# Units on both sides of every norm in halves of the tokens, low parts of the weights in place, three units resident

## The chip, the cores and the metric

The kernel runs on one core of a Trainium2 chip. The metric is the device time of one execution in microseconds (us). Five engines work side by side, each through its own list of instructions in order: TensorE (PE; its weight loads are shown apart as PEld), VectorE (DVE), ScalarE (ACT), GpSimd (POOL), and SyncE (SP), which here only starts DMAs.

## The reference

The input is one sequence of 512 tokens of width 1024. Three layers follow each other: layer a (forgetting attention, then a convolutional FFN), layer b (differential attention, then a convolutional FFN) and layer c (a gated mix of grouped attention and a state-space branch, then a gated FFN). Cut to the parts around the norms:

```
x = layer_norm(1.414 * x + attention_a(x));  x = layer_norm(1.414 * x + ffn(x))     # norms a0, f0
x = layer_norm(1.414 * x + attention_b(x));  x = layer_norm(1.414 * x + ffn(x))     # norms a1, f1
h = rms_norm(x) @ w_in_2                                                            # norm c0
x = x + rms_norm(mixed @ w_out)                                                     # norm m
h2 = rms_norm(x) @ w_gate_up;  x = x + rms_norm((silu(gate) * up) @ w_down)         # norms p and f
```

A layer norm subtracts the mean of a token over its 1024 values, divides by the root of the variance plus 1e-5, and applies a gain and an offset. An rms norm divides by the root of the mean square plus 1e-6 and applies a gain. There are eight norms, at six places: f1 is followed at once by c0, and m at once by p. The inputs and the result are float32.

## The kernel before

**Layout and precision.** An activation lies in SBUF as eight blocks of 128 features by 512 tokens. Each is split into a high part in a short float format (`XH`) and the rest (`XL`). A weight is split likewise: `RAW` is what the DMA brings, ACT rounds it to `HI` (L1530), and DVE or POOL subtracts to get `LO` (the helper at L1899 on DVE, at L2382 on POOL). A product is three matmuls: HI with XH, HI with XL, LO with XH. One such matmul has 128x128 stationary values and 512 moving columns, or 256 where the unit is of kind `mt` (tokens stationary, weights moving).

**Units.** All the weights are cut into units of up to 8 blocks of 128 rows by 256 columns (1 MB), taken in one fixed order (`unit_sequence`). Two units are resident: `RAW`, `HI` and `LO` have two buffers each (`i % 2`). SP loads unit i once HI and LO of unit i-2 are made (`load_raw`, L1195). While PE multiplies with unit i-1, unit i is split in up to four parts (`split_steps`, `part_step`); its first HI waits until PE is done with unit i-2.

**Order.** `agenda()` writes one list of steps. Each engine walks through it and picks out its own instructions, so this list is the order on every engine. `tick` counts matmul steps; it lets `chore()` advance background generators by one `yield`, and lets the attention run beside the units.

**Around a norm before.** The last units before a norm produce eight blocks `YH`, one after the other (`residual`, or the copy `cye`). After each, `accumulate` squares it on ACT (L1548) and adds the squares, and where there is a mean also the block, on POOL (L2402, L2404). When all are done, `statistics` sums over the features on PE: a matmul of a 128x128 piece with a single column, four token groups for each buffer (`stat0`); then small operations on DVE and ACT (`stat1`, `stat2`, L1937 to L1945, L1557 or L1560); then matmuls that spread the mean and the reciprocal over all partitions (`stat1`, `stat3`). Then for each block of 512 tokens: DVE subtracts and multiplies (L1953, L1956; for an rms norm one operation), ACT applies gain and offset (L1566) and rounds to `XH` (L1570), POOL makes `XL` (L2382). The first unit after the norm waits for XL block by block. At c0 and p a second norm of this kind comes before it. The last norm f ends with `fin`: DVE multiplies (L1970), DVE or POOL adds (L1978, L2504), SP stores.

In the trace all matmuls of the helper have line L1239, and the tiles tell them apart: `PS<-XH,HI` and the like are unit matmuls, `PS<-NEGC,FP` is the one that clears the bank of the sums and is the first of `stat0`, `PS<-FP,A_a` and `PS<-FP,SQ_a` are the sums, `PS<-FP,TN` the spreading. In the suffixes a stands for a0 and a1, f for f0 and f1, m, p and c for the norms of those names. A matmul of plain float32 values has two records.

```
def statistics(n, mean):
    at_bank(put("stat0", n, mean), 6)
    if mean:
        at_bank(put("stat1", n), 5)
    put("stat2", n, mean)
    put("stat3", n, mean)
def layer_norm(n, final=None):
    statistics(n, True)
    for j in range(8):
        s = put("ln", n, j)
```

## Time and profile before

| | us |
|---|---|
| median of 3 runs (lowest, highest) | 2441.58 (2437.21, 2452.46) |
| the profiled execution, whole | 2443.44 |
| its span, first to last instruction | 2441.6 |
| PE busy | 2254.6 (92%) |
| DVE busy | 1096.0 (45%) |
| ACT busy | 1001.4 (41%) |
| POOL busy | 974.8 (40%) |
| DMA queue q1 | 181.27 MB, 21.5% of 16 engines |

The profile is of one execution. Busy time is the union of an engine's instructions. A matmul's duration in it is longer than the distance to the next, because matmuls overlap; the rate of PE is read from start to start.

### The profile page before, as it was taken

What the parts mean: (1) busy time and instruction counts of PE and PEld (TensorE: products, weight loads), DVE (VectorE), ACT (ScalarE), POOL (GpSimd) and SP (SyncE); (2) the same over time, 40 slices, a digit from 0 to 9 for tenths busy, and PEclk for the clock granted to TensorE, in tenths of its full rate; (3) what the DMA queues carried; (4) which work ended last, traced back from release to release, by engine and by line L of the source; (5) the groups of instructions that cost most, each with busy time, mean ns of one, the idle gap of its engine ahead of it and who ended that gap; (6) DMA issues with size and microseconds to landing.
All of it is one profiled execution on the core that took longest, in us unless ns stands there. A gap on an engine that the chain in (4) does not pass through costs nothing.

```text
span 2441.6 us, 28073 instructions
## 1 busy us (share of the span) xinstructions
PE 2254.6 (92%) x10880; PEld 1841.6 (75%) x10880; DVE 1096.0 (45%) x1774; ACT 1001.4 (41%) x2015; POOL 974.8 (40%) x760
## 2 busy tenths in 40 slices
PE   7999999999979887999999789996899997999997
PEld 6778778888867776788888666664687885888886
DVE  3545555553345764555443333546545234232222
ACT  5665454443254553444442244443344234232222
POOL 3554644333455641644334351103423345232232
PEclk9999999999989998999999887997999997999998
DMA  4111222222212220222322111110012221222221
GB/s 152 51 65 58 70 87 91 100 101 95 97 61 75 77 83 18 70 101 90 104 97 95 59 46 35 35 35 18 18 44 95 86 104 52 104 87 104 97 95 50
DMA packets 29844, 183.07 MB, mean 75 GB/s; under 512 B 3984, under 2 KB 4112, under 8 KB 11920
## 3 DMA queue, kind: packets, MB, share of 16 engines
q1 hardware_dynamic: 29712, 181.27, 21.5%
q8 instruction: 87, 1.43, 0.2%
q14 instruction: 45, 0.37, 0.0%
HBM read 174.97 MB, written 2.10 MB: 73 GB/s over the span
## 4 chain that ended last, share of the span: by engine, by line
PE 84%; DVE 5%; ACT 4%; POOL 4%; issue 2%; DMA 1%; SPq 0%; POOLq 0%; ACTq 0%; DVEq 0%
PE PS L1239 82%; PE PS L1332 1%; POOL LO L2382 1%; POOL XL L2382 1%; PE PS L1442 1%; DVE bQS L1899 1%; DVE cCVT L2266 0%; DVE aQS L1899 0%; DMA RAW<-wall 0%; POOL A_p L2402 0%; POOL bROT L2430 0%; ACT bP L1739 0%; POOL A_c L2402 0%; PE PS L1380 0%; POOL bTQ L2435 0%
## 5 line engine op out<-in xcount | busy, mean ns | idle before, releaser
L2382 POOL TENSOR_TENSOR LO<-RAW,HI 128x512 fp32r<-128x512 f32 (+1 forms) x382 | 542.3, 1436 | 686.9 <-ACT HI L1530 686.9
L1239 PE MATMUL PS<-XH,HI 128*128 128x512 f32 (+1 forms) x1584 | 645.1, 407 | 40.7 <-POOL XL L2382 20.5
L1239 PE MATMUL PS<-XH,LO 128*128 128x512 f32 (+1 forms) x1584 | 628.1, 397 | 0.0
L1239 PE MATMUL PS<-XL,HI 128*128 128x512 f32 (+1 forms) x1584 | 628.1, 397 | 0.0
L1899 DVE TENSOR_TENSOR LO<-RAW,HI 128x512 fp32r<-128x512 f32 (+3 forms) x286 | 313.5, 1102 | 290.9 <-ACT HI L1530 290.7
L1530 ACT ACTIVATE HI<-RAW 128x512 fp32r<-128x512 f32 (+3 forms) x668 | 365.1, 608 | 170.6 <-PE PS L1239 167.2
L1239 PEld LDWEIGHTS PS<-XH,HI 128*128 128x128 f32 (+1 forms) x1584 | 303.7, 192 | 132.5 <-issue 57.3
L1239 PEld LDWEIGHTS PS<-XH,LO 128*128 128x128 f32 (+1 forms) x1584 | 302.9, 191 | 66.6 <-issue 1.1
L1239 PEld LDWEIGHTS PS<-XL,HI 128*128 128x128 f32 (+1 forms) x1584 | 304.2, 192 | 58.4 <-issue 1.0
L1239 PE MATMUL PS<-HH,HI 128*128 128x512 f32 x528 | 205.4, 389 | 0.0
L1239 PE MATMUL PS<-HL,HI 128*128 128x512 f32 x528 | 205.4, 389 | 0.0
L1239 PE MATMUL PS<-HH,LO 128*128 128x512 f32 x528 | 205.4, 389 | 0.0
L2418 POOL TENSOR_TENSOR UT<-UT 128x512 f32<-128x512 f32 x44 | 56.4, 1282 | 204.8 <-ACT UT L1591 204.8
L1239 PE MATMUL PS<-HI,XH 128*128 128x256 f32 (+1 forms) x416 | 125.7, 302 | 11.3 <-DVE aVL L1899 2.8
L1589 ACT ACTIVATE UT<-PS,SM 128x512 f32<-128x512 f32 x88 | 67.7, 772 | 131.4 <-PE PS L1239 131.4
L1239 PE MATMUL PS<-HI,XL 128*128 128x256 f32 (+1 forms) x416 | 119.4, 287 | 0.0
L1239 PE MATMUL PS<-LO,XH 128*128 128x256 f32 (+1 forms) x416 | 119.4, 287 | 0.0
L1239 PEld LDWEIGHTS PS<-HH,HI 128*128 128x128 f32 x528 | 99.1, 188 | 20.7
L1239 PEld LDWEIGHTS PS<-HH,LO 128*128 128x128 f32 x528 | 99.1, 188 | 20.6
L1239 PEld LDWEIGHTS PS<-HL,HI 128*128 128x128 f32 x528 | 99.1, 188 | 20.4
L1987 DVE SCALAR_TENSOR_TENSOR UT<-PS,SM,UT 128x511 f32<-128x511 f32 x88 | 65.4, 743 | 91.8 <-ACT UT L1589 91.8
L2424 POOL TENSOR_SCALAR aP<-aP,aRC 128x128 f32<-128x128 f32 (+1 forms) x64 | 69.3, 1084 | 92.0 <-DVE aRC L2068 91.8
(380 smaller groups left out, 3352.3 us busy)
## 6 DMA issues: line engine op xcount, KB each, us to landing
RAW<-wall SPq DMA_DIRECT2D x138, 1024.0 KB, 4.8
RAW<-wall SPq DMA_DIRECT2D x24, 896.0 KB, 4.4
bROT<-bTQ SPq DMA_DIRECT2D x64, 64.0 KB, 2.0
RAW<-wall SPq DMA_DIRECT2D x5, 512.0 KB, 3.2
XF<-xT SPq DMA_DIRECT2D x4, 512.0 KB, 6.0
outT<-XR SPq DMA_DIRECT2D x8, 256.0 KB, 2.0
FP<-cfp SPq DMA_DIRECT2D x1, 1024.0 KB, 6.8
MKF<-cmask SPq DMA_DIRECT2D x1, 704.0 KB, 11.4
```

The source lines that it names most:

```text
L1239: return e.matmul(out, a, b, start=start, stop=stop)
L1332: m = e.transpose(PS[bank][:, 128 * kb:128 * kb + 128], aP[:, 512 * (n % 4) + 128 * kb:512 * (n % 4) + 128 * kb + 128], IDN)
L1442: m = e.transpose(PS[bank][:, 128 * kb:128 * kb + 128], p[:, 128 * kb:128 * kb + 128], IDN)
L1530: act(HI[i % 2][:, c], RAW[i % 2][:, c], ACT.Copy).then_inc(SEM["hi"], 1)
L1589: act(x, PS[ag.tiles[t].bank][:, :], ACT.Identity, bias=col(f"cb{lay}", f), scale=col(f"cw{lay}2", f)).then_inc(SEM["ui"], 1)
L1899: return e.tensor_tensor(out, x, h.bitcast(F32), ALU.subtract)
L1987: e.scalar_tensor_tensor(out=x[:, 1:512], in0=ps[:, 0:511], scalar=col(f"cw{lay}1", f), in1=x[:, 1:512], op0=ALU.mult, op1=ALU.add).then_i ...
L2382: return e.tensor_tensor(out, x, h.bitcast(F32), ALU.subtract)
L2418: e.tensor_tensor(g, g, v, ALU.mult).then_inc(SEM["um"], 1)
L2424: e.tensor_scalar(p, p, aRC[:, n:n + 1], None, ALU.mult).then_inc(SEM["dg"], 1)
```

## The change

**Three units resident.** `LO` gets the addresses of `RAW`: the subtraction writes over its own input. The 48 KB hold three units then. SP loads unit i when PE is done with unit i-3, and the first HI of unit i waits for the same.

**Halves before a norm** (`ending`). The last units are multiplied for tokens 0 to 255 first, all of them, and then for tokens 256 to 511. At a0, a1 and m these are the last three units of four; at f0, f1 and f the last group of three long units (22 blocks of rows). A matmul has 256 moving columns there; both 128-column halves of a unit share one PSUM bank. In the long group the bank is cleared first by a matmul of float32 zeros with 512 columns (one for each half).

**Halves after a norm** (`beginning`). The first units take tokens 0 to 255 of all, then 256 to 511: two units in layers a and b (for b `bqk` 0 and `bv` 0, whose banks are now 2 and 3 in place of 0 and 1), three at c0 (`ck`, `cq` 0, `cq` 1) and three at p.

**The norm in between** (`chain`, `two_norms`) is a background generator, one for each half of the tokens, advanced by `chore()` as the units go on. `st0` sums over the features: POOL's running sums (`acc`) cover only the blocks before the halved units, and the halved blocks are summed by PE itself, each piece of 128x128 by a single-column matmul, for the squares and, where there is a mean, for the values. `stq` does so in c0 and p, for all eight blocks. `stb` spreads. Then pairs of blocks by 256 tokens are normalised (`lnp`, `lnr`, `rmp`, `n1`, `fin`), as many elements in an instruction as before.

`LATE` and `STATS` are the numbers of chore turns between the end of a half and its sums, and between the sums and the spreading. `HOLD` delays the splitting of the next unit. `XR` is moved to another address.

```diff
+HOLD = 16
+LATE = 4
+STATS = 4
...
+    def ending(n, groups, src, banks, evict, chain):
...
+        for f in range(2):
+            for (p, keys), bank in zip(groups, banks[f]):
...
+                    for k, q in rows:
+                        step_of("mh", t, kk + k, q)
+                        tick(0.5)
...
+                freed[bank] = evict(p, t, f)
+                put("acch", n, p, f)
+                at_slot(steps[-1], "P", p - 1, ("ssum", ("st0", n, f)))
+            together_chores.append(chain(f))
...
+    def beginning(units, last=False):
...
+        def known(kk, f):
+            while x_step[kk][f] is None:
+                assert chores or together_chores
+                chore()
...
+    def chain(n, f, mean, each, begun=False):
+
+        if not begun:
+            for _ in range(LATE):
+                yield
+            while bank_of_norm(n, f) in norm_at:
+                yield
+            norm_at.add(bank_of_norm(n, f))
+            s = put("st0", n, f)
+            at_bank(s, bank_of_norm(n, f))
+        put("st1", n, f)
+        for _ in range(STATS):
+            yield
+        s = put("stb", n, f)
+        b = bank_of_norm(n, f)
+        freed[b] = ("spr", s)
+        for p in range(4):
+            freed[b] = yield from each(f, p)
+        norm_at.discard(b)
...
+            s2 = put("sqp", n2, f, p)
+            at_slot(s2, "S", None, ("ssum", ("stq", n2, f, p)))
+            yield
+            yield
+            s2 = put("stq", n2, f, p)
...
+        ending(n, [(i, [(name, i)]) for i in (1, 2, 3)], src, [[2, 3, 4], [7, 0, 1]], residual_half(n), layer_norm(n))
...
+        ending(n, [(3, [("dn" + lay, 3, p) for p in range(3)])], "H" + lay, [[4], [7]], evict, chain)
...
+        beginning([("mm", ("bqk", 0), (128, 128), [0, 1], qk_evac(0)), ("mt", ("bv", 0), None, [2, 3], v_evac(0))])
...
+        beginning([("mm", ("ck", 0), (128,), [0], qk_evac(4)), ("mm", ("cq", 0), (128, 128), [1, 2], qk_evac(0)),
+                   ("mm", ("cq", 1), (128, 128), [3, 4], qk_evac(2))], last=True)
...
-    HI = [sb(f"HI{i}", 2048, F32R, base + 16 * K + 8 * K * i) for i in range(2)]
-    LO = [sb(f"LO{i}", 2048, F32R, base + 32 * K + 8 * K * i) for i in range(2)]
+
+    RAW = [sb(f"RAW{i}", 2048, F32, base + 8 * K * i) for i in range(3)]
+    LO = [sb(f"LO{i}", 2048, F32R, base + 8 * K * i) for i in range(3)]
+    HI = [sb(f"HI{i}", 2048, F32R, base + 24 * K + 8 * K * i) for i in range(3)]
...
+            if i >= 3:
+                e.wait_ge(*when_(ag.unit_end[i - 3]))
...
+                        if q == 0:
+                            mm(PS[T.bank][:, :], IDN, NEGC[:, 8:9].to_broadcast([128, 512]), True, False)
...
+            elif kind == "st0":
+                n, f = a
+                nb, mean = NORM[n], n in MEANED
+                e.wait_ge(*when("cd", "cst"))
+                mm(PS[bank][:, 0:4], IDN, NEGC[:, 8:12], True, False)
...
+                for c in range(2):
+                    t = slice(256 * f + 128 * c, 256 * f + 128 * c + 128)
+                    mm(PS[bank][:, c:c + 1], nb["A2"][:, t], MEAN[:, 0:1], False, False)
+                    if mean:
+                        mm(PS[bank][:, 2 + c:3 + c], nb["A1"][:, t], MEAN[:, 0:1], False, False)
+                for p in pairs_of[n]:
+                    if mean:
+                        e.wait_ge(*y_half(n, p, f))
+                        for q in range(2):
+                            for c in range(2):
+                                y = blk(YH, 2 * p + q)[:, 256 * f + 128 * c:256 * f + 128 * c + 128]
+                                mm(PS[bank][:, 2 + c:3 + c], y, MEAN[:, 0:1], False, False)
+                    e.wait_ge(*when("sq", "acch", n, p, f))
+                    for q in range(2):
+                        for c in range(2):
+                            y = nb[f"P{p - 1}"][:, 256 * q + 128 * c:256 * q + 128 * c + 128]
+                            done = mm(PS[bank][:, c:c + 1], y, MEAN[:, 0:1], False, p == pairs_of[n][-1] and q == 1 and c == 1)
...
+            elif kind == "stb":
...
+                if n in MEANED:
+                    for c in range(2):
+                        mm(ps[:, 128 * c:128 * c + 128], SUMS[f][:, 2 + c:3 + c].to_broadcast([128, 128]), IDN)
+                for c in range(2):
+                    done = mm(ps[:, 256 + 128 * c:384 + 128 * c], RSD[f][:, c:c + 1].to_broadcast([128, 128]), IDN)
```

## Rows read from the trace of the kernel before

**Rows 1.** The page: busy time by engine; PE's clock in 40 slices.
```profile
PE 2254.6 (92%) x10880; PEld 1841.6 (75%) x10880; DVE 1096.0 (45%) x1774; ACT 1001.4 (41%) x2015; POOL 974.8 (40%) x760
...
PEclk9999999999989998999999887997999997999998
```

**Rows 2.** Timeline around norm f0: start us, length us, engine, line, tiles, [idle <-releaser].
```profile
672.01 0.39 PE L1239 MATMUL PS<-HH,HI 128*128 128x512 f32 x1
...
676.09 0.39 PE L1239 MATMUL PS<-HH,HI 128*128 128x512 f32 x1
...
676.77 0.28 PE L1239 MATMUL PS<-NEGC,FP 128*128 128x8 f32 x2
...
692.55 0.69 DVE L1953 TENSOR_TENSOR T_f<-PS,YH 128x512 f32<-128x512 f32 x1 [3.00 <-PE PS L1239]
...
695.55 2.65 POOL L2382 TENSOR_TENSOR XL<-T_f,XH 128x512 fp32r<-128x512 f32 x2 [14.18 <-ACT XH L1570]
...
696.97 0.77 PE L1239 MATMUL PS<-XH,HI 128*128 128x512 f32 x1 [4.45 <-POOL XL L2382]
...
701.37 0.44 PE L1239 MATMUL PS<-XL,HI 128*128 128x512 f32 x1
```

**Rows 3.** Timeline of PE around norms f1 with c0, and m with p.
```profile
1379.38 0.28 PE L1239 MATMUL PS<-NEGC,FP 128*128 128x8 f32 x2
...
1416.76 0.77 PE L1239 MATMUL PS<-XH,HI 128*128 128x512 f32 x1 [2.95 <-POOL XL L2382]
```
```profile
2029.53 0.28 PE L1239 MATMUL PS<-NEGC,FP 128*128 128x8 f32 x2
...
2058.00 0.77 PE L1239 MATMUL PS<-XH,HI 128*128 128x512 f32 x1 [2.95 <-POOL XL L2382]
```

**Rows 4.** Timeline of PE around norms a0 and a1.
```profile
302.56 0.28 PE L1239 MATMUL PS<-NEGC,FP 128*128 128x8 f32 x2
302.97 1.95 PE L1239 MATMUL PS<-FP,A_a 128*128 128x1 f32 x16
304.77 1.18 PE L1239 MATMUL PS<-FP,YH 128*128 128x1 f32 x8
...
316.22 0.76 PE L1239 MATMUL PS<-XH,HI 128*128 128x512 f32 x1 [4.46 <-POOL XL L2382]
```
```profile
1006.57 0.28 PE L1239 MATMUL PS<-NEGC,FP 128*128 128x8 f32 x2
...
1018.35 0.76 PE L1239 MATMUL PS<-XH,HI 128*128 128x512 f32 x1 [4.46 <-POOL XL L2382]
```

**Rows 5.** Timeline at the end, behind the last unit matmul; the last addition.
```profile
2419.65 0.28 PE L1239 MATMUL PS<-NEGC,FP 128*128 128x8 f32 x2
...
2428.08 0.75 DVE L1970 SCALAR_TENSOR_TENSOR YH<-YH,SM,PS 128x512 f32<-128x512 f32 x1 [2.17 <-PE PS L1239]
...
2437.95 1.26 POOL L2504 TENSOR_TENSOR XR<-XR,YH 128x512 f32<-128x512 f32 x1 [1.29 <-DVE YH L1970]
```

**Rows 6.** Windows: stretch, us, busy by engine, PEclk, DMA share, GB/s.
```profile
304.00:305.00 1.00, 1.00 (x12) 1.00 (x11) 0.17 (x1) 0.78 (x2) 0.00 (x0) 1.00 0.59 246
...
306.00:307.00 1.00, 1.00 (x6) 1.00 (x6) 0.00 (x0) 0.33 (x2) 0.00 (x0) 0.50 0.00 0
```

**Rows 7.** Timeline of PE: matmuls of 256 columns (unit bv), and of float32.
```profile
918.98 0.28 PE L1239 MATMUL PS<-LO,XH 128*128 128x256 f32 x1
...
920.05 0.28 PE L1239 MATMUL PS<-LO,XH 128*128 128x256 f32 x1
```
```profile
1699.14 1.95 PE L1239 MATMUL PS<-FP,cBC 128*128 128x512 f32 x4 [0.88 <-DVE FP L2329]
```

**Rows 8.** Waits of PE from 705 to 735, behind norm f0: sum, times, longest.
```profile
PE PS L1239 <- DVE bVL L1899: 5.4, 1, 5.4
PE PS L1239 <- ACT bTQ L1707: 2.0, 1, 2.0
```

**Rows 9.** Waits of ACT over the whole span: sum, times, longest.
```profile
ACT HI L1530 <- PE PS L1239: 167.2, 26, 7.6
```

More of the change, by code:

```diff
@@ L163 @@
     "res": (("res", 1),),
[L164 to L170 removed]
+    "resh": (("res", 1),),
+    "acch": (("sq", 1),),
+    "sqp": (("sq", 1),),
+    "stq": (("ssum", 1),),
+    "st0": (("ssum", 1),),
+    "stb": (("spr", 1),),
+    "lnp": (("lt", 1), ("la", 1), ("xh", 1), ("xl", 1)),
+    "lnr": (("lt", 1), ("la", 1)),
+    "rmp": (("lt", 1), ("xh", 1), ("xl", 1)),
     "ue": (("ui", 2), ("ud", 2), ("us", 1), ("um", 1), ("hh", 1), ("hl", 1)),
@@ new lines, in beginning @@
+    def beginning(units, last=False):
+        ts = []
+        def known(kk, f):
+            while x_step[kk][f] is None:
+                assert chores or together_chores
+                chore()
+        held = None
+        for f in range(2):
+            for q, (kind, key, widths, banks, evac) in enumerate(units):
+                if not f:
+                    i = take(key)
+                    if last and q == len(units) - 1:
+                        held, due[0] = due[0], None
+                    rows = [(i, k) for k in range(places[key][1])]
+                    ts.append((len(tiles), rows))
+                    if kind == "mm":
+                        for j, w in enumerate(widths):
+                            tiles.append(Tile(rows, sum(widths[:j]), w, banks[j], "X"))
+                    else:
+                        for c in range(4):
+                            tiles.append(Tile(rows, 0, places[key][2], banks[c % len(banks)], "X", c))
+                            tiles[-1].half = c // 2
+                t0, rows = ts[q]
+                if kind == "mm":
+                    for kk in range(len(rows)):
+                        known(kk, f)
+                        for j in range(len(widths)):
+                            step_of("mm", t0 + j, kk, f)
+                            tick(0.5)
+                    if f:
+                        for j in range(len(widths)):
+                            evac(j, t0 + j)
+                else:
+                    for c in (2 * f, 2 * f + 1):
+                        for kk in range(len(rows)):
+                            known(kk, f)
+                            step_of("mt", t0 + c, kk)
+                            tick(0.5)
+                        freed[tiles[t0 + c].bank] = evac(c, t0 + c)
+                if held is not None and f and q == len(units) - 2:
+                    due[0], due[1], held = held, 0.0, None
@@ L512, in rms_apply @@
-    def rms_apply(n):
-        statistics(n, False)
-        for j in range(8):
-            x_step[j] = put("rms", n, j)
-            freed[6] = ("lt", x_step[j])
+        s = put("acc", n, j, mean)
+        if j:
+            at_slot(s, "S", None, ("ac", s))
+    def chain(n, f, mean, each, begun=False):
[16 more added lines that the diff above has]
+        norm_at.discard(b)
@@ new lines, in bank_of_norm, with normed, each, layer_norm @@
+    def bank_of_norm(n, f):
+        return 6 - (f if n not in ("c0", "p") else 1 - f)
+    def normed(n, kind):
+        def each(f, p):
+            s = put(kind, n, f, p)
+            at_slot(s, "T", None, ("xl", s))
+            x_step[2 * p][f] = x_step[2 * p + 1][f] = ("xl", s)
+            yield
+            yield
+            return ("lt", s)
+        return each
+    def layer_norm(n):
+        return lambda f: chain(n, f, True, normed(n, "lnp"))
+    def two_norms(n, n2):
+        def each(f, p):
+            if n == "f1":
+                s = put("lnr", n, f, p)
+                at_slot(s, "T", None, ("la", s))
+            else:
+                s = put("n1", n, f, p)
+            s2 = put("sqp", n2, f, p)
+            at_slot(s2, "S", None, ("ssum", ("stq", n2, f, p)))
+            yield
+            yield
+            s2 = put("stq", n2, f, p)
+            if p == 0:
+                norm_at.add(bank_of_norm(n2, f))
+                at_bank(s2, bank_of_norm(n2, f))
+            return ("lt", s)
+        def both(f):
+            yield from chain(n, f, n == "f1", each)
+            yield from chain(n2, f, False, normed(n2, "rmp"), True)
+        return both
@@ new lines, in scalar @@
+                dst = buf(n, "S", step) if j else NORM[n]["A2"]
+                act(dst[:, :], blk(YH, j), ACT.Square).then_inc(SEM["sq"], 1)
+            elif kind == "acch":
+                n, p, f = a
+                e.wait_ge(*y_half(n, p, f))
+                if ag.slot_free[step] is not None:
+                    e.wait_ge(*when_(ag.slot_free[step]))
+                act(by2(buf(n, "P", step)[:, :]), pair(YH, p, f), ACT.Square).then_inc(SEM["sq"], 1)
+            elif kind == "sqp":
+                n, f, p = a
+                e.wait_ge(*(when("la", "lnr", "f1", f, p) if n == "c0" else when("n1", "n1", "m", f, p)))
+                if ag.slot_free[step] is not None:
+                    e.wait_ge(*when_(ag.slot_free[step]))
+                act(by2(buf(n, "S", step)[:, :]), pair(XR, p, f), ACT.Square).then_inc(SEM["sq"], 1)
+            elif kind == "st0":
@@ L1578, in scalar @@
                 act(blk(YH, j), PS[ag.tiles[t].bank][:, :], ACT.Copy).then_inc(SEM["cye"], 1)
+            elif kind == "cyeh":
+                n, p, t, f = a
+                e.wait_ge(*when_(ag.tiles[t].full))
+                act(pair(YH, p, f), by2(PS[ag.tiles[t].bank][:, :]), ACT.Copy).then_inc(SEM["cye"], 1)
             elif kind == "ue":
```

549 lines of the change are left out of this document (303 added, 246 removed).

## The prediction

> **What bounds the kernel now.** I read the page first. PE is busy 92% of the span and the other engines 40 to 45% [rows 1]; the clock line shows nines but for a few slices, so PE runs near its full clock of 2.4 GHz and nothing else is close to being the bound. So time can come only from PE: its holes, its slow stretches, and the work given to it. The rate of that work is read in the timeline from start to start: six times three matmuls of 512 columns start between 672.01 and 676.09, which is 0.227 us each [rows 2]. PE is dense like this over all the FFN parts.
>
> Next, the timeline of PE at each norm. From the row that clears the bank of the sums to the first `PS<-XH,HI` there pass 13.7 us at a0 and 11.8 at a1 [rows 4], 20.2 at f0 [rows 2], 37.4 at f1 with c0 and 28.5 at m with p [rows 3]: 111.6 us. Behind it the clock is low for a while: at f0 ten matmuls take 4.40 us (696.97 to 701.37) and not 2.27, so 2.1 us are lost [rows 2]; at five places 10.6. At the end 22.0 us lie between the last unit matmul and the end of the span, 2441.6 - 2419.65 [rows 5]. Sum of what the norms cost: **144.2 us**. One more hole hangs on the place behind f0: PE waits 2.0 us for a bank that holds `bqk` 0 and 5.4 us for one that holds `bv` 0 [rows 8].
>
> **The change, part by part.**
>
> *Removed.* If everything were covered, the 122.2 us at five places go, and the end is worked out below. The two waits behind f0, 7.4 us, should go: `bv` gets banks 2 and 3, and `bqk` 1 then takes banks that were emptied a whole half unit earlier. Bounds 0 (DVE is late for another bank) and 10 (the slow clock behind the wait goes too). I take 7.4.
>
> *Narrower matmuls.* Nine matmuls of 256 columns start between 918.98 and 920.05, in 1.07 us: 0.119 each [rows 7]. Two of them against one of 0.227 cost 0.011 more. Halved are, before norms, 3 units x 48 matmuls at a0, a1 and m (432) and 22 blocks x 2 x 3 = 132 at f0, f1 and f (396); behind norms 96 at each of a0 and a1, 48 for `bqk` 0, 120 at c0, 144 at p (504). `bv` has 256 columns already. 1332 x 0.011 = **14.7 us**. Bounds: 0, and 1332 x 0.025 = 33 if short accumulations run worse than `bv`.
>
> *Sums on PE.* This is the part that costs. A single-column matmul of float32 takes (304.77 - 302.97) / 8 = 0.225 us [rows 4], as long as a whole unit matmul of 512 columns, since its price is the weight load. Before, POOL added seven of eight squares and PE needed 16 sums and a clearing matmul for a layer norm, 9 for an rms norm. Those are inside the holes counted above. Now `st0` needs, for each half at a0 and a1, 1 + 4 + 3 x 8 = 29; at f0 and f1 1 + 4 + 8 = 13; at m 1 + 2 + 3 x 4 = 15; `stq` at c0 and p 1 + 4 x 4 = 17; f 7. `stb` adds 4 for a layer norm and 2 for an rms norm; I price these as the others (a bound above is 0.35). For both halves: a0 and a1 66 each, f0 and f1 34 each, c0 and p 38 each, m 34, and f's first half 9. 319 x 0.225 = **71.8 us**, on PE's path because the lists run in order. The clearing with 512 float32 columns: two matmuls are the four records of 1.95 us [rows 7], some 0.95 each after the overlap; two at f0, f1 and f each, 6 x 0.95 = **5.7 us**.
>
> *The end.* From the first multiplication of `fin` at 2428.08 to the last addition's end at 2439.2 pass 11.1 us for eight blocks [rows 5]. The second half is four pairs, the same work by halves: 5.6 saved. Sums and spreading halve too, about 2.9 less. 22.0 - 8.5 = **13.5 us** remain. Bounds 11 and 17.
>
> *Waits that stay.* One turn of `chore` is two steps, six matmuls of 256 columns: 0.71 us. From the spreading to the first XL the old chain needs 692.55 to 696.97, 4.4 us [rows 2], and POOL makes an XL in 1.33 (2.65 for two), DVE needs two operations of 0.69 for a pair, ACT about as much. So pairs come every 1.5 to 1.7 us. Behind a0: five turns 3.6, sums 6.5, four turns 2.9, spreading 0.9, 4.4: 18.3 us, against a first half of two units of 11.4 plus the 7.4 that PE itself spends on sums and spreading. It fits; a pair is used up in 1.4 us, so 2 us at a0 and a1 each and 1 at f0. At c0 it does not fit. `stq` of a pair stands only two turns (1.4 us) behind the pair's `lnr`, yet DVE, ACT and the square need 3.2: 1.8 us of standing in each half, with the unit matmuls queued behind it on PE. Then `ck` is narrow, a pair feeds 0.7 us of work while pairs come every 1.5, and the spreading comes right ahead of the units: some 4.6 us in each half. Together 12.8. At m with p the halves are longer; 4.4. Sum **22 us**, bounds 8 and 45: DVE, ACT and POOL also split the next units meanwhile, and each waits in order.
>
> *The clock.* In the trace PE goes down to 1.2 GHz with no hole ahead: between 302.97 and 308 it does single-column matmuls one after the other and is busy throughout, and the granted clock is 1.00 in 304 to 305 and 0.50 in 306 to 307 [rows 4, 6]. So it falls about 3 us into such a run. `st0` at a0 and a1 is a run of 29 x 0.225 = 6.5 us in each half. Its rest of 3 us would take twice as long, and a little is lost behind it: 3.6 us, four times, 14.4. At f0, f1 and m the runs are 2.9 to 3.4 us, and it will fall in some of six: 4. Behind the standing at c0 and p, 5.6. Sum **24 us**, bounds 0 and 40. The Trainium skill, "TensorE: Matmul & The Clock Gate", section "Why this matters for your kernels", asks only that there be no idle gaps between bursts of matmuls. By that rule dense sums would keep the clock, and the change would remove what lowered it; this trace does not agree at a0, where PE was not idle.
>
> *Three units resident.* ACT waits 167.2 us for PE in front of HI [rows 9], but all 26 waits are of up to 7.6 us beside dense matmuls, and PE waited for no LO worth naming. Loads of 1 MB have a whole unit's time as before. Subtracting in place is as much work. Nothing: bounds -5 and +5.
>
> *Sum.* Removed 122.2 + 22.0 + 7.4 = 151.6. Added 14.7 + 71.8 + 5.7 + 13.5 + 22 + 24 = 151.7. Net 0.1 on the profiled execution's 2443.4; that stands 1.9 above the median of 2441.6, so the forecast is **2442 us**.
>
> **The rivals.**
>
> *A. Dense sums keep the clock* (also the skill's rule above). For it: at f0 the slow matmuls stand right behind holes [rows 2], which the change fills, and the units are dense on both sides of each sum; against it the rows at a0 [rows 4, 6]. Then 24 us fewer: 2418, and with waits at their lower bound 2404.
>
> *B. PE stands at the sums in every half: slower.* The mechanism is the order of the list: a sum or a spreading put at a fixed number of turns stands ahead of the unit matmuls on PE, and DVE, ACT and POOL come to it late because the splitting of units, now at twice the rate (5.7 us a unit and not 10.9), is queued ahead of it. It decides once squares come over 3.6 us behind the end of a half. There are 14 half chains ahead of f; at 2.3 us each, standing and clock, 32 more: 2474. For it: a unit's split is four subtractions as wide as the one that takes POOL 1.33 us [rows 2], two of them or more on POOL, so POOL alone spends 2.7 of those 5.7 us, beside the XL. Against: they are 40 to 45% busy on the whole [rows 1].
>
> *C. The halves do not overlap with the chain.* The beginning of a unit pumps `chore` until its block is known, and this empties the turns without any matmul between. It can only bite at c0 and p, since elsewhere the turns suffice. Price 10 more at each: 2462.
>
> **Chances.** Forecast 0.48, A 0.24, B 0.16, C 0.12. The likeliest gives 2442. Its own range is 2425 to 2460 (the bounds of the waits and the clock half used). The range for 8 in 10 reaches to both sides: **2406 to 2472**. A measurement of this kernel can tell about 1% from no change. Faster by over 1% (under 2417): half of A, a lower tail of the forecast and of an end that shrinks more, 0.29. Slower by over 1% (over 2466): B mostly, part of C and of the forecast's upper tail, 0.23. Within 1%: 0.48.
>
> **What would show it.** In the changed profile: PE's busy share rises to some 96% with the span unchanged. Single-column matmuls number over twice as many, at 0.225 us where the clock is full. At a0 and a1 the windows show a clock of 0.50 inside or just behind `st0`, with PE busy. The time from the last full-width matmul of `ao` 0 to the first of `up` 2, less its unit matmuls at 0.119, is above the 15 us that norm a0 cost before: the layer norms behind attention lose some 10 us each, f0 wins about 17, m with p a few, and the end 6 to 8. PE waits for POOL XL only at `ck`. The forecast is wrong if the clock stays at 1.00 through `st0`, if the waits of PE in the transitions sum to over 45 us, or if the matmuls of 256 columns start more than 0.125 us apart.

## The result, and the profile after

The change makes the kernel slower: 2489.03 us against 2444.22 for the kernel before in the same session (medians of four runs each; 2478.86 to 2489.78 and 2437.21 to 2452.46). The ratio is 1.017, with a 95% interval of 1.013 to 1.0215. On a second chip it was 2487.46 against 2436.59, ratio 1.0207 (1.0178 to 1.0236). The forecast was 2442 in a range up to 2472; the loss is 46 us of span in the profiled executions (2487.8 against 2441.6). One of the nine executions of a later run, `h1_both`, took 2627.63 us at a granted clock of 0.82 and is left out of that run's numbers.

The page of the kernel after: busy time by engine, PE's clock, the chain of waits by engine.

```profile
span 2487.8 us, 31338 instructions
PE 2332.1 (94%) x12565; PEld 1972.8 (79%) x12576; DVE 1101.3 (44%) x1826; ACT 1014.5 (41%) x2061; POOL 917.1 (37%) x718
...
PEclk9999999999999898899999886996899999999999
...
PE 84%; DVE 5%; ACT 4%; POOL 3%; issue 2%; DMA 0%; another core or an unknown queue 0%; SPq 0%; POOLq 0%; ACTq 0%; DVEq 0%
```

Against [rows 1], PE is busy 77.5 us more and the span is 46 longer, so about 31 us of holes went. They were filled with work, and with slow work. The time that PE is busy at half clock grew from 185.7 to 222.2 us, which costs half of the difference, 18; so 59 of the 77.5 us are work at full clock, and 59 + 18 - 31 is the 46. The table says where: I compared the starts of the same marks in both traces (first `PS<-aOH,HI`, first `PS<-HH,HI` of each FFN, called `HH` 0 to 2, first and last `bQS`, first `cMXH`, the end). The third column is the prediction's own working, its terms sorted by place.

| stretch | after minus before, us | by the prediction's terms |
|---|---|---|
| norm a0 | +14.5 | +10.9 |
| norm f0, to the first `bQS` | -9.6 | -15.8 |
| attention b, first to last `bQS` | +5.9 | 0 |
| norm a1 | +14.5 | +12.8 |
| f1, c0 and part c up to `cMXH` | +22.7 | -1.7 |
| m and p | +1.4 | -2.7 |
| f and the end | -3.1 | -3.1 |

They sum to 46.3 (the kernel after is 0.2 ahead at the first mark) and 0.4. Half of the miss is one row, f1 with c0 and part c.

**Norm a0.** The timeline of PE in the kernel after, then windows of the same stretch (stretch, us, busy by engine, PEclk, DMA share, GB/s).

```profile
292.18 0.28 PE L1441 MATMUL PS<-NEGC,FP 128*128 128x4 f32 x2
292.31 1.03 PE L1441 MATMUL PS<-FP,A_a 128*128 128x1 f32 x8
...
295.00 1.55 PE L1441 MATMUL PS<-FP,YH 128*128 128x1 f32 x8
296.41 1.84 PE L1441 MATMUL PS<-FP,P_a 128*128 128x1 f32 x8
...
299.82 1.84 PE L1441 MATMUL PS<-FP,P_a 128*128 128x1 f32 x8
```
```profile
290.00:295.00 5.00, 5.00 (x47) 5.00 (x45) 0.20 (x1) 2.12 (x3) 0.00 (x0) 1.00 0.01 3
295.00:300.00 5.00, 5.00 (x27) 5.00 (x27) 0.00 (x0) 0.00 (x0) 0.00 (x0) 0.53 0.00 0
300.00:303.00 3.00, 3.00 (x15) 3.00 (x16) 0.65 (x4) 0.30 (x1) 0.00 (x0) 0.50 0.00 0
303.00:306.00 3.00, 3.00 (x17) 3.00 (x17) 0.26 (x1) 0.00 (x0) 0.00 (x0) 0.57 0.01 3
```

Two records are one sum. Four sums take 0.90 us from 292.31 and 1.70 from 296.41. PE has no hole in this stretch, it is busy 16 of 16 us, and the granted clock goes from 1.00 to 0.50 some 3 us into the run of 29 sums, as it did behind [rows 4]; it stays there for 10.2 us, beyond the end of the sums (in the second half for 6.8). This is what the prediction priced at 3.6 us in each half.

**Norm c0.** The same two views of the kernel after.

```profile
1407.15 0.28 PE L1441 MATMUL PS<-NEGC,FP 128*128 128x4 f32 x2
1409.18 1.05 PE L1441 MATMUL PS<-FP,S_f 128*128 128x1 f32 x8 [1.74 <-ACT S_f L1795]
...
1411.69 1.70 PE L1441 MATMUL PS<-FP,S_f 128*128 128x1 f32 x8
...
1415.96 1.70 PE L1441 MATMUL PS<-FP,S_f 128*128 128x1 f32 x8
...
1430.32 0.35 PE L1441 MATMUL PS<-XH,HI 128*128 128x256 f32 x1 [2.80 <-POOL XL L2646]
...
1434.59 0.55 PE L1441 MATMUL PS<-XH,HI 128*128 128x256 f32 x1 [3.32 <-POOL XL L2646]
```
```profile
1405.00:1410.00 5.00, 3.26 (x30) 3.17 (x29) 3.97 (x7) 2.60 (x5) 0.00 (x0) 1.00 0.28 98
1410.00:1415.00 5.00, 5.00 (x31) 5.00 (x31) 1.27 (x2) 4.27 (x9) 0.00 (x0) 0.65 0.00 0
1415.00:1420.00 5.00, 5.00 (x25) 5.00 (x25) 0.00 (x0) 0.00 (x0) 0.00 (x0) 0.50 0.55 187
1420.00:1425.00 5.00, 5.00 (x25) 5.00 (x25) 0.49 (x2) 0.57 (x2) 0.00 (x0) 0.50 0.06 23
```

The waits are where the prediction put them: PE stands 1.74 us for the square of the first pair (the prediction said 1.8), and for POOL's XL behind the spreading. From 1395 to 1474 they sum to 12.9 us (9.4 for XL, 3.5 for squares), against 12.8 predicted. The clock is what differs. Behind the stand of 1.74 us it falls, and then PE does 13.7 us of dense work of layer 1 at half speed, unit matmuls with three groups of sums between them, with no hole in it (x25 records in 5 us; 47 in the window at full speed above).

**Behind f0.** PE in attention b, then ACT at the same time, in the kernel after.

```profile
761.76 0.23 PE L1441 MATMUL PS<-MK 128*128 128x128 bf16 x1
768.52 1.01 PE L1441 MATMUL PS<-bQS 128*128 128x384 f32 x2 [6.53 <-ACT bP L1993]
```
```profile
741.53 0.63 ACT L1766 ACTIVATE HI<-RAW 128x512 fp32r<-128x512 f32 x1 [4.42 <-DMA RAW<-wall]
...
765.08 1.27 ACT L1979 ACTIVATE bQS<-bTQ 64x512 fp32r<-64x512 f32 x2 [4.55 <-POOL bTQ L2695]
766.36 1.28 ACT L1993 ACT_TABLE_LOAD   x1
767.66 0.37 ACT L1993 ACTIVATE bP<-PS,bST 128x128 f32<-128x128 f32 x1
```

The two waits of [rows 8] are gone, and a new one of 6.53 us stands 35 us later, for the first exponential. Two things ahead of it on ACT could be the cause: the stand of 4.42 us for a load, and the one of 4.55 us for POOL in the conversion of the rope. Run `h3_load_first` moves the first.

**The end.** Last sums and last addition of the kernel after, the partner of [rows 5].

```profile
2474.80 0.28 PE L1441 MATMUL PS<-NEGC,FP 128*128 128x4 f32 x2
...
2483.80 1.26 POOL L2764 TENSOR_TENSOR XR<-XR,YH 128x512 f32<-128x512 f32 x1 [1.41 <-DVE YH L2237]
```

From the last unit matmul to the end of the span pass 13.1 us (2487.8 - 2474.7), where 13.5 were predicted.

### The profile page after: what moved, and what is told of

Its sections match the earlier page's. It is cut to its first block, busy times and chain, and to the rows that moved or that the text cites. A ratio compares the mean times of both kernels' runs of the same rounds, so it can differ in the third digit from the quotient of the medians.

```text
span 2487.8 us, 31338 instructions
## 1 busy us (share of the span) xinstructions
PE 2332.1 (94%) x12565; PEld 1972.8 (79%) x12576; DVE 1101.3 (44%) x1826; ACT 1014.5 (41%) x2061; POOL 917.1 (37%) x718
## 4 chain that ended last, share of the span: by engine, by line
PE 84%; DVE 5%; ACT 4%; POOL 3%; issue 2%; DMA 0%; another core or an unknown queue 0%; SPq 0%; POOLq 0%; ACTq 0%; DVEq 0%
PE PS L1441 82%; POOL LO L2646 1%; PE PS L1568 1%; PE PS L1678 1%; POOL XL L2646 1%; DVE aQS L2153 0%; ACT bP L1993 0%; DVE LO L2153 0%; ACT HI L1766 0%; DVE bQS L2153 0%; PE PS L1616 0%; POOL A_f L2666 0%; ACT bQS L1979 0%; ACT T_a L1815 0%
## 5 line engine op out<-in xcount | busy, mean ns | idle before, releaser
L1441 PE MATMUL PS<-XH,HI 128*128 128x512 f32 (+2 forms) x1752 | 675.2, 385 | 40.1 <-POOL XL L2646 20.1
L1441 PE MATMUL PS<-XL,HI 128*128 128x512 f32 (+2 forms) x1752 | 657.0, 375 | 0.0
L1441 PE MATMUL PS<-XH,LO 128*128 128x512 f32 (+2 forms) x1752 | 656.7, 375 | 0.0
L1441 PEld LDWEIGHTS PS<-XH,HI 128*128 128x128 f32 (+1 forms) x1752 | 337.7, 193 | 117.4 <-issue 39.4
L1766 ACT ACTIVATE HI<-RAW 128x512 fp32r<-128x512 f32 (+3 forms) x668 | 365.9, 607 | 97.4 <-DMA RAW<-wall 96.9
L1441 PEld LDWEIGHTS PS<-XH,LO 128*128 128x128 f32 (+1 forms) x1752 | 337.6, 193 | 58.5 <-issue 1.1
L1441 PEld LDWEIGHTS PS<-XL,HI 128*128 128x128 f32 (+1 forms) x1752 | 338.3, 193 | 51.8 <-issue 1.0
L1441 PE MATMUL PS<-HH,HI 128*128 128x512 f32 (+1 forms) x660 | 235.7, 357 | 3.3 <-POOL LO L2646 3.2
L1441 PE MATMUL PS<-HL,HI 128*128 128x512 f32 (+1 forms) x660 | 231.9, 351 | 0.0
L1441 PE MATMUL PS<-HH,LO 128*128 128x512 f32 (+1 forms) x660 | 231.8, 351 | 0.0
L1441 PEld LDWEIGHTS PS<-HH,HI 128*128 128x128 f32 x660 | 128.2, 194 | 21.0 <-POOL LO L2646 3.6
L1441 PEld LDWEIGHTS PS<-HL,HI 128*128 128x128 f32 x660 | 128.2, 194 | 16.9 <-issue 1.4
L1441 PEld LDWEIGHTS PS<-HH,LO 128*128 128x128 f32 x660 | 128.2, 194 | 15.4
L1842 ACT ACTIVATE UT<-PS,SM 128x512 f32<-128x512 f32 x88 | 67.5, 771 | 126.4 <-PE PS L1441 126.4
```

What stands on the lines that cost most here:

```text
L1441: return e.matmul(out, a, b, start=start, stop=stop)
L1766: act(HI[i % 3][:, c], RAW[i % 3][:, c], ACT.Copy).then_inc(SEM["hi"], 1)
L1842: act(x, PS[ag.tiles[t].bank][:, :], ACT.Identity, bias=col(f"cb{lay}", f), scale=col(f"cw{lay}2", f)).then_inc(SEM["ui"], 1)
```

## The experiments

Every ratio is to the kernel before, run on the same chip in the same session. "The marks" are those of the table above.

**e1_resident: three units resident, alone.** In the kernel before, three buffers each of RAW and HI, LO in RAW's place, and the waits that go with them:

```
-                    e.wait_ge(s_raw[i % 2], 16 * (i // 2 + 1))
-                    if i >= 2:
-                        e.wait_ge(*when_(ag.unit_end[i - 2]))
+                    e.wait_ge(s_raw[i % 3], 16 * (i // 3 + 1))
+                    if i >= 3:
+                        e.wait_ge(*when_(ag.unit_end[i - 3]))
```

> The kernel before with the three resident units alone: LO written over RAW, loads and the first HI of unit i waiting for PE's end of unit i-3; no halves. Theory (residency is free): within 5 us of before, 2439 to 2449. Rival (ACT now stands at HI for the load, in front of its other work, and this is what the attention parts of the changed kernel lost): 8 to 15 us slower, with ACT's waits for the DMA of RAW near 97 us as in the changed kernel.

Measured: 2444.08 us, ratio 1.0026 (1.0002 to 1.005), span 2442.3 against 2441.6. All the marks lie within 3 us of those before. By the profiles this part costs 0.6 us, by the ratio 6 (0.5 to 12), by the medians 10 (2434.2 before in that session). The rival's sign is there: ACT waits 108.9 us for the loads of `RAW` (96.9 in the kernel after). Its 8 to 15 us are neither shown nor excluded. It is not what made most of the 46.

**e2_narrow: only narrower matmuls.** In the kernel before, all 66 `up` units as matmuls of 256 columns, 3168 becoming 6336 (`three` is the kernel's three matmuls on a range of columns):

```
+                    if ag.order[i][0] in ("up0", "up1", "up2"):
+                        m = three(kk, w, slice(0, 256), start, stop)
+                        if stop:
+                            for q in range(8):
+                                m = three(q, slice(q * n + T.c, q * n + T.c + T.w), slice(256, 512), q == 0, q == 7)
```

> The kernel before with all 66 `up` units in matmuls of 256 columns, tokens 0 to 255 of a tile first and then the rest: 3168 matmuls become 6336, nothing else is changed. My prediction's term (0.011 us for each halved matmul): 35 us more, 2479. Rival (the matmuls in the halves cost 0.1235 us, 0.020 each): 63 us more, 2507. If width cost nothing: 2444.

Measured: ratio 1.0231 (1.0186 to 1.0275), 56 us, close to the rival's 63 and not to 35. Over 3168 that is 0.018 us for each halved matmul; by the marks the three layers cost 17.4, 19.3 and 15.6 us over 1056 each, 0.015 to 0.018. The prediction took 0.011 from nine starts in a row of `bv`. Within a row it was nearly right: in `up0` of e2 twenty starts from 400.06 take 2.40 us, 0.120 each, so a halved matmul costs 0.013. The rest comes between the rows (layer 0 has 2.1 us more holes). In the kernel after, the unit matmuls of 256 columns stand 0.123 us apart on average (clock and holes taken out). So the term of 14.7 us is 17 by the rows and **24** by e2's ratio.

**e3_fewer_sums: fewer sums at a0 and a1.** In the kernel after; the sums of the first two halved pairs of a0 and a1 are left out of the statistics, 13 in place of 29 in each half:

```
                 for p in pairs_of[n]:
+                    if n in ("a0", "a1") and p != pairs_of[n][-1]:
+                        continue
```

> The changed kernel, leaving out of the sums of norms a0 and a1 the halved blocks of units 1 and 2 (16 of 29 single-column matmuls in each half; the values of these norms are then those of fewer blocks). Theory (each sum costs 0.225 us of PE, and a run of 29 also brings the clock down over dense work): 64 x 0.225 = 14.4 us for the sums and some 10 for the clock, 24 less than the changed kernel, 2465. Rival (the clock falls for another reason, the sums alone count): 14 less, 2475. Rival (sums hide under other waits): under 6 less.

Measured: 2469.25 us, ratio 1.0134 (1.0108 to 1.016), between my theory's 2465 and the rival's 2475. Over the kernel before of its own session it is 35 us, where the kernel after is 45 and 51 (`e0_after_again`): 10 to 16 us less. The sums themselves are 64 x 0.225 = 14.4, so the times alone don't show that the clock counts. The trace does: half clock over matmuls is 3.4 us at each of a0 and a1, where the kernel after has 17.1 and 13.7, worth 12. By the marks of this execution, which was 8 us faster than the run's median, a0 costs 1.0 us over the kernel before and not 14.5, a1 2.7 and not 14.5: 25.3 us less. Windows of e3, for comparison with those of a0 above:

```profile
295.00:300.00 5.00, 5.00 (x37) 5.00 (x37) 0.65 (x4) 0.30 (x1) 0.00 (x0) 0.79 0.00 2
300.00:303.00 3.00, 3.00 (x22) 3.00 (x22) 1.38 (x2) 0.03 (x1) 0.00 (x0) 0.77 0.17 22
303.00:306.00 3.00, 3.00 (x27) 3.00 (x27) 2.81 (x5) 2.00 (x4) 0.00 (x0) 1.00 0.81 328
```

The clock still falls, for 3.4 us and not 10.2.

**e4_probe: the same sums in dense work.** In the kernel before, single-column matmuls put between the unit matmuls of `up`: four runs of 29 in layer 0, four of 13 in layer 1, sixteen of 4 in layer 2 (they add work and take none away):

```
+    if name in plan and j in plan[name][1] and T.c == 0 and kk in plan[name][2]:
+        for _ in range(plan[name][0]):
+            mm(PS[6][:, 0:1], IDN, MEAN[:, 0:1], True, True)
```

> The kernel before with single-column float32 matmuls of a constant put between the dense unit matmuls of the FFNs, results unused: in `up0` one run of 29 in each of four units, in `up1` one run of 13 in each of four, in `up2` four runs of 4 with six unit matmuls between them in each of four units. Theory: a run of 29 brings the clock down every time (about 6.5 us at full clock, 10 with the fall), a run of 13 sometimes (2.9 us, up to 5), runs of 4 among dense matmuls never. Rival (density keeps the clock as long as PE has no hole): 1.00 throughout, and 0.225 us for each of the 232, 52 us in all.

The timeline of PE at a run of 29, one of 13 and one of 4 (here the run of 29 shows 38 of its 58 records in this row, the others stand ahead of it).

```profile
376.64 7.13 PE L1239 MATMUL PS<-FP 128*128 128x1 f32 x38
383.63 0.77 PE L1239 MATMUL PS<-XH,HI 128*128 128x512 f32 x1
...
384.63 0.63 PE L1239 MATMUL PS<-XH,LO 128*128 128x512 f32 x1
...
1128.91 0.63 PE L1239 MATMUL PS<-XH,LO 128*128 128x512 f32 x1
...
2173.79 0.95 PE L1239 MATMUL PS<-FP 128*128 128x1 f32 x8
...
2174.92 0.39 PE L1239 MATMUL PS<-XL,HI 128*128 128x512 f32 x1
```

And windows around the first run of 29: dense from end to end, and the clock at half, 1.2 GHz, from inside the run until 10.2 us later.

```profile
374.00:377.00 3.00, 3.00 (x27) 2.88 (x26) 1.46 (x2) 0.78 (x1) 0.00 (x0) 1.00 0.97 322
377.00:380.00 3.00, 3.00 (x20) 3.00 (x20) 0.30 (x2) 1.55 (x3) 1.27 (x1) 0.65 0.07 27
380.00:383.00 3.00, 3.00 (x16) 3.00 (x16) 2.45 (x3) 1.79 (x4) 2.17 (x2) 0.50 0.00 0
383.00:386.00 3.00, 3.00 (x10) 2.52 (x11) 0.00 (x0) 0.00 (x0) 0.84 (x1) 0.50 0.40 87
```

Measured: 2515.0 us in one execution, 73 us over the kernel before by the mark `HH` 2. A run of 29 costs 11.8 us (6.5 of its own), a run of 13 some 5.7 (2.9 of its own; the unit matmuls behind it are 0.43 apart and not 0.227 for 3.4 us), a run of 4 costs 0.90, its own time, and the clock stays at 1.00 in all sixteen. So the price of a sum in a long run is not 0.225 us. It is 0.225 in a run of 4, 0.44 in a run of 13 and 0.41 in a run of 29. And the clock fell at every one of the four runs of 13, 2.5 to 3.3 us behind its start, twice just as the run had ended; the prediction had said "some of six".

**e0_after_again** is the kernel after, unchanged.

> The changed kernel once more, as the base for the three runs beside it: 1.017 of the kernel before, 35 to 50 us over it.

Measured: 2487.46, ratio 1.0207 (1.0178 to 1.0236), 51 us over the kernel before by the medians. Its marks agree with the first trace within 3 us, so single differences of 1 to 3 us between two traces mean nothing here. In part c they can be larger. Windows from the first `cP` to the first `cMXH`, a stretch with no sums of a norm in it: the kernel before, e2 (whose code is that of the kernel before there), the kernel after.

```profile
1427.55:1986.01 558.46, 514.21 (x2606) 389.71 (x2607) 253.09 (x402) 215.31 (x479) 153.42 (x128) 0.93 0.15 53
1466.99:2013.14 546.15, 496.43 (x2594) 381.46 (x2606) 253.85 (x402) 215.18 (x479) 153.14 (x128) 0.96 0.16 54
1474.03:2033.83 559.80, 513.83 (x2592) 396.36 (x2603) 249.68 (x400) 213.72 (x475) 150.26 (x125) 0.91 0.14 51
```

The same code takes 12 us more or less here, with its clock: half clock over matmuls is 64.2 us in the kernel before, 62.3 in e1, but 30.7 in e2 and 34.2 in e4.

**e5_few_stq: fewer sums at c0 and p.** In the kernel after; three of four sums of each pair but the last are left out of the second norm's statistics, 8 in place of 17 in each half:

```
-                for q in range(2):
-                    for c in range(2):
+                for q in range(2 if p == 3 else 1):
+                    for c in range(2 if p == 3 else 1):
```

> The changed kernel, leaving out 9 of the 17 single-column sums in each half at c0 and at p (pairs 1 to 3 of 4 are summed over one of their four pieces; the values of these norms are then those of fewer blocks). Theory (sums cost 0.225 us each and bring PE's clock down over halved units at c0): 36 x 0.225 = 8 us and 8 to 10 more for the clock, 16 to 18 less than the changed kernel. Rival (the clock there falls behind the standing at `stq`, which stays): 8 less and the same slow stretches at 1411 to 1425 us.

Measured: 2471.52, 16 us below the kernel after (ratio 1.0136, 1.0105 to 1.0167), as my theory said. The sums left out are 36 x 0.225 = 8.1; the rest is clock. The stand of 1.74 us is still there, and the clock does not fall behind it.

**e7_late_stq: the sums of c0 and p one pair later.** In the kernel after, complete; `stq` of a pair is put behind the application of the next one:

```
-            s2 = put("stq", n2, f, p)
+            for q in ((p - 1,) if 0 < p < 3 else (2, 3) if p == 3 else ()):
+                ...
+                s2 = put("stq", n2, f, q)
```

> The changed kernel with each `stq` put one pair of blocks later, so that PE doesn't stand for the squares. Theory (1.7 us of standing in each of the four halves at c0 and p, and the clock behind it): 7 to 12 less than the changed kernel. Rival (the last sum of a half comes as late as before, so the wait moves to the spreading or to the first XL): within 3.

Measured: 2473.13, 14 us below the kernel after (ratio 1.0143, 1.0113 to 1.0173), more than the 7 to 12 of my theory. PE with e7 at c0, then windows of it:

```profile
1410.69 1.05 PE L1445 MATMUL PS<-FP,S_f 128*128 128x1 f32 x8 [0.30 <-ACT S_f L1799]
...
1417.77 0.95 PE L1445 MATMUL PS<-FP,S_f 128*128 128x1 f32 x8
```
```profile
1409.00:1414.00 5.00, 4.70 (x42) 4.61 (x40) 3.71 (x6) 4.90 (x10) 0.00 (x0) 1.00 0.00 0
1414.00:1419.00 5.00, 5.00 (x44) 5.00 (x44) 0.43 (x1) 2.40 (x7) 0.74 (x1) 1.00 0.58 210
```

There are as many sums as in the kernel after, at the same distance, but the stand ahead of them is 0.30 us and not 1.74, and the clock stays at 1.00 where it was 0.50. By the marks part c costs 17 us less, and m with p 3 more. The waits that went are 2.9 us (squares, 3.5 to 0.6) and 1.4 for XL; the half clock that lay over matmuls between the marks `HH` 1 and the first `cP` went from 34.9 to 16.4 us, worth 9.2. In e5 it went to 16.9. Either cure, fewer sums or no stand, saves about the same clock: so long a fall needs both together. The three traces in which this place is as in the kernel after (it, `e0_after_again` and e3) each have 34 to 35 us of half clock over matmuls here.

**e6_r_squares: cheap sums.** In the kernel after, complete; the squares of the halved blocks are rounded to fp32r, so their sums run in one pass, with two moving columns (the second column of `MEANR` is zero):

```
-  done = mm(PS[bank][:, c:c + 1], y, MEAN[:, 0:1], False, ...)
+  done = mm(PS[bank][:, 2 * c:2 * c + 2], y, MEANR[:, 0:2], False, ...)
```

> The changed kernel with the squares of the halved blocks rounded to the short float format and summed by one-pass matmuls with two columns (one zero): 160 of the sums have one record in place of two. Theory (the price is the float32 weight load, made twice): 0.11 us less each, 18 us, and 10 to 15 more where shorter runs no longer bring the clock down: 28 to 33 less than the changed kernel. Rival (these small matmuls take as long in one pass): no gain.

The timeline of PE at a0 in e6: four sums of squares are four records, and start 0.45 us ahead of the next group, while four sums of values in float32 need 0.89.

```profile
292.15 1.03 PE L1442 MATMUL PS<-FP,YH 128*128 128x1 f32 x8
293.04 0.58 PE L1442 MATMUL PS<-MEANR,P_a 128*128 128x2 f32 x4
293.49 1.08 PE L1442 MATMUL PS<-FP,YH 128*128 128x1 f32 x8
```

Measured: 2461.58, 26 us below the kernel after (ratio 1.0097, 1.0065 to 1.0128), the largest single gain and just short of the 28 to 33 of my theory.

**Four more, to find a version that beats both.** Each adds one edit to the one ahead of it. `h1_both` is e6 with e7. `h2_whole_end` has the units ahead of a0 and a1 whole again, `h3_load_first` moves one load, `h4_whole_m` has the edit of h2 for `co` as well, so that the units ahead of m are whole too. `both_halves` runs the chain of the first half and then that of the second.

```
 h2: -        ending(n, [(i, [(name, i)]) for i in (1, 2, 3)], ...)
     +        for i in (1, 2, 3):
     +            for j, t in enumerate(lin_fm((name, i), src)): residual(n, 2 * i + j, t)
     +        together_chores.append(both_halves())
 h3: +            first = ag.order[i - 3] == ("bqk", 0)
     +            if first:
     +                load_raw(i)
                  if ag.order[i - 3][0] == "bqk":
                      rotate(ag.order[i - 3][1])
```

> The kernel after with the last two edits together: squares of the halved blocks in the short format (sums in one pass), and the sums of c0 and p one pair later. My theory (the two cures act on different things: the first on the length of the runs of sums everywhere, the second on PE standing for squares at c0 and p): the gains add, less the part of the clock at c0 and p that both remove (some 4 us): 26 + 14 - 4 = 36 us below the kernel after, ratio to the kernel before about 1.005. The rival (both saved the same time, the half clock behind the sums of c0 and p): no better than the first alone, ratio 1.009 to 1.010.

Measured: 2458.09 (median of eight), ratio 1.0068 (1.0045 to 1.0091), against 1.0097 (1.0065 to 1.0128) for e6 alone. By these the second cure adds 6 to 7 us to the first, but the intervals overlap, so the rival's nothing is not excluded. That both act in part on the same half clock at c0 fits: e6 alone brings it from 34.9 to 17.2 us.

> As h1_both, but at a0 and a1 the three units ahead of the norm are whole again, with their squares added up by POOL as in the kernel before, so that each half needs 5 sums in place of 29; the units behind the norm stay halved. My theory: at each of a0 and a1 it takes away 144 x 0.018 = 2.6 us of narrow matmuls, 24 sums of 0.225 and 24 of half that (8.1 us) and about 5 us of half clock, and brings back a hole of some 12 us ahead of the first pair: 4 us less each, 8 us below h1_both, ratio 1.002. The rival (a hidden chain is worth more than its sums): the hole comes back at its full size and the clock falls in it, 3 to 6 us more at each, ratio 1.008 to 1.010.

Measured: ratio 1.0080 (1.0058 to 1.0102); the ratios alone don't tell it from h1. By the marks a0 costs 12.9 us over the kernel before (7.0 in h1), and a1, from the last `bQS` to `HH` 1, 16.2 (13.5 in h1): the rival, by 2.7 to 6 us each. PE at a0 in h2 shows why:

```profile
309.97 1.87 PE L1456 MATMUL PS<-FP,A_a 128*128 128x1 f32 x8 [4.60 <-POOL A_a L2685]
...
319.81 0.55 PE L1456 MATMUL PS<-XH,HI 128*128 128x256 f32 x1 [4.72 <-POOL XL L2663]
...
341.82 0.39 PE L1456 MATMUL PS<-XH,HI 128*128 128x256 f32 x1 [4.64 <-POOL XL L2663]
```

The hole ahead of the first half is back, in two parts of 4.6 and 4.7 us, and the second half's chain, which the first half of the next units was to cover, leaves one more of 4.6.

> As h2_whole_end, with one line of SP's list moved: the load of bqk 2 is issued ahead of the rotation of bqk 0 and not behind it. In the kernel after, ACT stood 4.4 us at HI for that load, with a conversion of the rope queued behind it, and PE then waited 6.5 us. My theory: this wait is what took the place of the 7.4 us that were removed behind f0; it goes, 4 to 6 us less between the first and the last turn of bQS, ratio 0.998 to 1.000. The rival (the rotation's own transfers, now behind 1 MB on the queue, come later and PE waits as long for them): no change, ratio as h2_whole_end.

Measured: ratio 1.0081 (1.0054 to 1.0108), no change; from the first to the last `bQS` 6.0 us over the kernel before, 6.2 in h2. ACT's stand for the load is gone, and PE in h3 waits as long:

```profile
764.77 1.01 PE L1460 MATMUL PS<-bQS 128*128 128x384 f32 x2 [6.51 <-ACT bP L2014]
```
```profile
761.33 1.27 ACT L2000 ACTIVATE bQS<-bTQ 64x512 fp32r<-64x512 f32 x2 [4.53 <-POOL bTQ L2716]
762.62 1.28 ACT L2014 ACT_TABLE_LOAD   x1
```

Moving the load did not help. That is not proof that the load played no part: ACT's next wait for POOL's rotated block grew to 7.2 us (6.0 in the kernel after), as the rival said it would. What stands right ahead of the exponential on ACT in both is the conversion of the rope, which waits 4.5 us for POOL, and then a table load of 1.28 us. In the kernel before the same conversion waited as long (4.61 us at 755.76), no table load stood behind it, and PE came to it later. Whether the wait would go with another order of ACT's list was not tried.

> As h3_load_first, with the three units ahead of m whole as well, squares added up by POOL, 3 sums in place of 15 in each half. My theory: at m halving costs little (144 x 0.018 = 2.6 us, 24 sums in one pass 2.7, a little clock) against a hole of some 10 us that it covers, so this loses 3 to 6 us: ratio 0.002 above h3_load_first. The rival (whole units ahead of a norm are better wherever the sums can be added up on POOL): 2 to 4 us less.

Measured: ratio 1.0114 (1.0087 to 1.014), 9 us slower than h3 by the medians (the intervals overlap); by the marks m and p together cost 9.7 us more. Halving ahead of m is worth that much with sums in one pass, more than my theory's 3 to 6.

None of these beats the kernel before. The best by its ratio, h1, is 0.45 to 0.9% slower; h2 and h3 can't be told from it.

## Why the prediction was wrong

The account was the right one in kind: holes closed against work added on PE. Its removed terms held. The holes at the norms went but for the waits that were foreseen, the end is 13.1 us (13.5 said), and the waits at the norms are 27.3 us: 1.6 at a0, 4.8 at f0, 1.6 at a1, 12.9 at f1 with c0, 6.4 at m with p, where 22 were said. The work was right too, by an estimate from the traces. Its added terms are 92.2 us, and the holes and the end that it removed hold some 33 us of old sums at full clock, which leaves 59, as measured. So the 46 us are clock and holes. What failed, by size:

- **The clock: "some of six: 4" and "behind the standing at c0 and p, 5.6".** The step took the clock's fall in a run of sums from [rows 4, 6] and priced it mostly inside the run. The probe shows that it lasts beyond the run: behind 13 sums for 3.2 to 3.8 us, once 6, and so 2.8 us are lost for each. At a0 and a1 the term was sound: PE had 17.1 us of half clock over matmuls at a0 and 13.7 at a1, worth 15.4 us, where 14.4 were said. At c0 it was not. From `HH` 1 to the first `cP` the kernel after has 34.9 us of half clock over matmuls; with the stand at the squares taken away (e7) it has 16.4, so the stand and the groups of sums behind it cost 9.2 us at c0 alone, where the prediction had 5.6 for c0 and p together.
- **The clock over all of part c.** From `HH` 1 to the first `cMXH` PE's holes shrink from 66.0 to 60.5 us, and half clock over matmuls grows from 85.2 to 126.4, which is 20.6 us. The terms gave 2.0 more (4.1 added, 2.1 removed), and the hole of 37.4 that they removed held another 16.1 us of half clock, worth 8. By the same count the clock was missed by some 27 us here, all of the 24.4 by which this row was missed. A third of the 20.6 lies ahead of the first `cP`. The other 13.6 us lie behind it, where no norm sums: 64.2 us of half clock before, 91.5 after, and no run took that away (81 to 107 in all the others made from the kernel after). The code of the kernel before had 31 to 64 in four traces. Why the changed kernel has more is open. One difference is that it puts unit matmuls worth some 11 us ahead of the first `cP` (150 of 256 columns, where there were 27 of 512), so that fewer stand beside the attention; this was not tried.
- **Waits behind f0, 7.4 removed.** They were removed, and 5.9 us of it came back 35 us later, since PE was then ahead of the rope. The prediction asked what is late next at every other place, and not here.
- **Waits that stay, 22.** 27.3; the excess is at f0 (4.8, said 1) and m with p.
- **Narrower matmuls, 14.7.** Measured 17 to 24 (e2), inside its bounds. Since the work as a whole came out right, other work took as much less; which is not told apart.
- **Three units resident, nothing.** 0.5 to 12 us (e1), so its bound of +5 is not confirmed.

In sum, by whole traces: half clock over matmuls costs 18 us more than before, where the terms, counted the same way (24 added, 10.6 removed, and the half of the 48.5 us that stood inside the removed holes), gave 11 less: 29 us. PE's holes shrank by 31 us where the terms gave some 48: 17 us, of which 5 are waits at the norms, 6 attention b, and the rest small waits that were not followed. These are estimates from one pair of traces, and the half clock of part c alone moves such a pair by up to 17 us.

**The rivals.** A (dense sums keep the clock, 2418) is refuted: in the windows of e4, PE is busy for 12 of 12 us and the clock still halves. The Trainium skill, "TensorE: Matmul & The Clock Gate", section "Why this matters for your kernels", asks for no idle gaps between bursts of matmuls; here the clock fell with no gap at all, so that does not suffice. B (2474) named the side and the place, PE standing for squares with unit matmuls queued behind, at 2.3 us in each half; in the trace such stands are 3.5 us at c0 and 2.1 at m in all, and it is the clock behind the ones at c0 that costs. That its 2474 is the nearest of the four is in part luck, since only the two halves at c0 of its fourteen behave so. C is not seen at c0: between the groups of sums at c0 stand twelve unit matmuls each, two turns as planned.

Of the signs that the prediction listed, PE's share rose to 94% (96 said), the clock is 0.50 inside the sums of a0, and the matmuls of 256 columns are 0.123 us apart, just short of the 0.125 that would have called it wrong. The sum of the waits, 27.3, stayed under its 45 as well. Two of its signs by place failed: m with p was to win a few us and lost 1.4, and f0 was to win 17 and won 9.6. The list had no line for half clock over unit matmuls, and there the time went.

## What to carry to other kernels

Before a hole on PE is filled with many small matmuls, put a few runs of them into dense work and read how long the unit matmuls behind each run stay slow: that is the price, and here it was nearly twice the run's own time from 13 sums on and nothing extra for 4. So sum in one pass, or in groups of four, and put a step that reads another engine's result one turn later than it seems to need. Leaving the sums to another engine was tried only with whole units ahead of the norm (h2, h4), and cost more there by the marks. When a wait is removed, look for the chain that was hidden beside it. And before a difference between two profiles is explained, look how far two traces of the same code lie apart in that stretch.

## What the runs showed of the hardware

A busy PE can lose its clock. 29 float32 matmuls of one column in a row, with dense 512-column matmuls on both sides and no hole, bring the granted clock from 2.4 to 1.2 GHz for 10.2 us; 13 do it for 3.4 (once 6.8); 4 never did in sixteen. At a0 and a1, where halved unit matmuls follow, 29 did it for 10.2 once and for 6.8 three times. At c0 groups of four sums between twelve unit matmuls kept the clock when PE stood 0.30 us ahead of them (e7) and lost it for 13.7 us when it stood 1.74; with single sums in place of the first groups behind the same stand (e5) it stayed. A float32 matmul of one column is two records and 0.225 us, and with fp32r squares one record and 0.11. A float32 matmul of 512 columns that clears a bank took 0.86 us, where 0.95 was said. Halving an fp32r matmul of 512 columns cost 0.013 us within a row and 0.018 on average.
